# First merge step's gate products placed in the last prompt unit and the dilated decode; gates first in the merge; norm sums in other PSUM banks

## The chip, the cores and the metric

The kernel runs on one core of a Trainium2 chip. The metric is the device time of one execution in microseconds (us), the median of three runs. All matmuls are float32.

## What the reference computes

Two decoder layers, each over 256 prompt rows and 32 decode rows (8 samples of 4 new tokens). The kernel carries all 288 rows as one block of columns, so nearly every weight product is a matmul of 128 x 128 weights with 288 columns. Cut to what matters here, a layer is:

```
z = x @ w_in + b_in                      # queries, keys, values, merge gates
y_nsa = nsa_mixer(...)                   # 8 heads, 512 columns
y_dil = dilated_mixer(...)               # 3 groups of 4 heads, 256 columns
gm = sigmoid(g_merge)                    # last 2 x 1024 columns of z
mixed = gm[:, :, 0] * (y_nsa @ w_br_nsa) + gm[:, :, 1] * (y_dil @ w_br_dil)
x = layer_norm(ALPHA * x + mixed @ w_o, ln1_g, ln1_b)
h = square(relu(x @ w_ff1))
x = layer_norm(ALPHA * x + h @ w_ff2, ln2_g, ln2_b)
```

The gate columns of z need only the layer's input x. The branch products need y, which is there when attention has ended.

## The kernel before, in words

The five engines run programs of their own, written out by hand in one function (`build`), in fixed order, and they meet at semaphores that count up. Nothing plans the order at run time: an engine that reaches a wait stands until the count is there, and everything behind it in its program stands too. TensorE (`block.tensor`) does all products and transposes. ScalarE and VectorE take results out of PSUM. SyncE (`block.sync`) issues the weight loads one after another, each behind a wait for its buffer; GpSimd issues pages and values of the cache, and ScalarE issues stores and the copies of old cache rows into the new caches (`roll`, line 815).

**Weights** go through `w_ring`, four slots of 8 KB a partition. Unit u uses slot u % 4, and `free_of` (line 427) is SyncE's wait before it loads unit u: it waits for the last product that read the unit four before. Units 20 to 35 are the merge, 36 to 39 `w_o`, from 40 on the feed-forward weights. **Keys** of the decode caches go through `kv_ring`, two buffers of the same size.

**Around the change** the order on TensorE within a layer is this.

- Lines 1905 to 1916: the prompt units n = 16 to 23 of dilated attention. Each has scores (`p_scores`), transposes of the probabilities (`p_transpose`, line 1798) and values (`p_values`, line 1815). Between them run the 14 rounds of dilated decode keys (`d_round`, line 1878), which transpose keys out of `kv_ring`. VectorE's `dil_bias` (line 1356) comes before its `p_scale(23)`, so the transposes of unit 23 wait for it.
- Lines 1917 to 1947: the dilated decode. Ten transposes of its probabilities (`dlogit`) into banks 0 to 2, which ScalarE and VectorE copy to `pt`; then 160 recorded matmuls of probabilities with values into bank 6 (called P·V below); ScalarE copies the result out; four transposes put it in bank 7, and eight small copies by ScalarE put it into `yT`.
- Lines 1950 to 1960: the merge, a loop over p = 0 to 3 of 256 columns each. Within p there are four parts: w = 0 (`w_br_nsa`, 8 matmuls), w = 1 (`w_br_dil`, 4), w = 2 and w = 3 (the two gates, 16 each). Part w reads ring slot w and writes banks 2w and 2w + 1. ScalarE copies the branches and takes the tanh of the gates, VectorE joins them into `mixed` (lines 1396 to 1404).
- `wo` (line 1961): the eight output chunks of `mixed @ w_o`, for rows 0 to 143 (h = 0), then for rows 144 to 287 (h = 1), in banks 2 to 7. The sums of the layer norm (`mean`, `squares`, lines 1524 and 1538) are matmuls with ones, in banks 0 and 1 for the first norm (`LN_MEAN`, `LN_SQ`, line 80).
- `ff1_part` (line 1987): the first eight chunks of the feed-forward, by halves, in the order of `FF1_FIRST` = (4, 5, 6, 7, 2, 3, 0, 1), since banks 0 and 1 still hold the norm sums. Chunk c reads ring slot c // 2.

SyncE's order there: the last keys (line 638), the merge units 20 to 35 in order (lines 640 to 643), `w_o` (line 644), then `w_ff1`. The loop of the merge on TensorE before:

```
with pe.Fori(0, 4) as p:
    for w, (nk, k0, src) in enumerate(((4, 0, yT), (2, 4, yT), (KC, 0, xT), (KC, 0, xT))):
        pe.wait_ge(w_rdy[w].sem, ...)
        pe.wait_ge(mg_a.sem, mg_a.after(l, 4 * p + (w - 3)))
        for c in range(2):
            for k in range(nk):
                last = mm(bank(2 * w + c, 0, TOK), slot(w, nk, 256)[:, k, ...], src[:, k0 + k], k == 0, k == nk - 1)
        last.then_inc(mg_mm.sem, 1)
```

Of the kernel before, what the change touches and what calls it, by code (L numbers as in the profile page):

```python
# [79 lines left out]
LN_MEAN, LN_SQ = (0, 4), (1, 5)  # L80
HALF = (slice(0, TOK // 2), slice(TOK // 2, TOK))
FF1_FIRST = (4, 5, 6, 7, 2, 3, 0, 1)
# [6 lines left out]
NO_UNIT = (5, 8, 9, 19)  # L89
# [139 lines left out]
def build(nc, x_prompt, x_sample, cache_nsa_kv, cache_nsa_win, cache_dil_w128, cache_dil_w512, cache_dil_w2048,  # L229
# [11 lines left out]
    with ExitStack() as ctx:  # L241
# [134 lines left out]
        kv_rdy = [sig(f"kv_{s}", 16 * sum(KV_DMAS[s::2])) for s in range(2)]  # L376
        toep_rdy = [sig(f"dil_toep_{x}", 32) for x in range(2)]
# [42 lines left out]
        def _(sp):  # L420
# [6 lines left out]
            def free_of(l, u):  # L427
# [17 lines left out]
                elif v < U_MERGE:  # L445
                    b = v - (U_MERGE - W_SLOTS)
                    sp.wait_ge(dd_pv.sem, dd_pv.after(l, 4 * (b % 2) + b // 2 + 1))
                    sp.sem_inc(sp_steps, 1)
                elif v < U_WO:
                    sp.wait_ge(mg_mm.sem, mg_mm.after(l, v - U_MERGE + 1))  # L450
                    sp.sem_inc(sp_steps, 1)
                elif v < U_FF1:
                    sp.wait_ge(wo_mm.sem, wo_mm.after(l, 2 * (v - U_WO) + 2))
                    sp.sem_inc(sp_steps, 1)
                else:
                    raise ValueError(v)
# [10 lines left out]
            for l in range(layers):  # L467
# [19 lines left out]
                def kv_free(k):  # L487
                    v = k - 2
                    if v < 0:
                        sp.wait_ge(dd_pv.sem, dd_pv.after(l, v + 1))  # L490
                        sp.sem_inc(sp_steps, 1)
# [148 lines left out]
                for u in range(U_MERGE, U_MERGE + 4):  # L640
                    merge_unit(u)
                for u in range(U_MERGE + 4, U_WO):
                    merge_unit(u)
# [49 lines left out]
        def _(pool):  # L693
# [4 lines left out]
            for l in range(layers):  # L698
# [36 lines left out]
                def load_kv(k):  # L735

                    if k == 1:
                        pool.wait_ge(dd_pv.sem, dd_pv.after(l, 0))
# [55 lines left out]
        def _(act):  # L794
# [17 lines left out]
            for l in range(layers):  # L812
# [197 lines left out]
                A.copy(kt[:, 0, :], bank(6)).then_inc(dd_o.sem, 1)  # L1010
                act.wait_ge(dd_ot.sem, dd_ot.after(l, 1))

                o_v = bank(7).rearrange("p (q c b e s t) -> p q c b e s t", q=2, c=2, b=4, e=2, s=4)
# [64 lines left out]
        def _(dve):  # L1078
# [47 lines left out]
            for l in range(layers):  # L1126
# [279 lines left out]
                def wo_keep(h, c):  # L1406
                    done, cols = (wo_first, wo_mm)[h], HALF[h]
                    dve.wait_ge(done.sem, done.after(l, c + 1))
                    V.scalar_tensor_tensor(out=res[:, c, cols], in0=xT[:, c, cols], scalar=ALPHA, in1=bank(2 + c % 6, 0, TOK)[:, cols],  # L1409
# [55 lines left out]
        def _(pe):  # L1465
# [82 lines left out]
            for l in range(layers):  # L1548
# [376 lines left out]
                last.then_inc(dd_pt.sem, 1)  # L1925
                pe.wait_ge(dd_pta.sem, dd_pta.after(l, 1))
                pe.wait_ge(dd_ptd.sem, dd_ptd.after(l, 1))
                for par in range(2):
                    for q in range(4):
                        pe.wait_ge(dv_rdy[2 * q + par].sem, dv_rdy[2 * q + par].after(l, 64))  # L1930
                    for m in range(10):
                        for q in range(4):
# [3 lines left out]
                            out = bank(6, 256 * par, 256, pair.start, pair.stop)  # L1936
                            if m < 7:
                                mm(out, pt[:, m, pair], v[:, 256 * m:256 * m + 256], m == 0, False)
                            else:
                                a = 768 + 512 * (m - 7) + 256  # L1940
                                last = mm(out, pt[0:ND, m, pair], tm[0:ND, 2, a:a + 256], False, m == 9)
                                if m == 9:
                                    last.then_inc(dd_pv.sem, 1)
                pe.wait_ge(dd_o.sem, dd_o.after(l, 1))
                for k in range(4):
                    last = tr(bank(7, 128 * k, 128), kt[:, 0, 128 * k:128 * k + 128])
                last.then_inc(dd_ot.sem, 1)


                pe.wait_ge(dd_y.sem, dd_y.after(l, 1))  # L1950
                pe.wait_ge(dn_y.sem, dn_y.after(l, 2))
                pe.sem_inc(pe_steps, 1)
                with pe.Fori(0, 4) as p:
                    for w, (nk, k0, src) in enumerate(((4, 0, yT), (2, 4, yT), (KC, 0, xT), (KC, 0, xT))):
                        pe.wait_ge(w_rdy[w].sem, w_rdy[w].after(l, 16 * p + 16 * (w_loads(w, U_MERGE) + 1)))
                        pe.wait_ge(mg_a.sem, mg_a.after(l, 4 * p + (w - 3)))
                        for c in range(2):
                            for k in range(nk):
# [136 lines left out]
```

## Time and profile before

| What | us |
|---|---|
| Median of three runs | 1618.79 (1618.61 to 1619.01) |
| The profiled execution | 1611.5 |
| Span of the profiled execution, first to last instruction | 1609.8 |
| TensorE busy with matmuls | 1520.3 (94% of the span) |
| VectorE busy / ScalarE busy | 361.7 / 347.9 |

The profile shows one execution. An engine's timeline gives start, duration, engine, line, operation, out<-in and count of merged instructions, and in brackets how long the engine stood idle before and what ended it. One float32 matmul of the program shows as two records on TensorE (a float32 transpose as one). Because matmuls are pipelined, the duration of a row reaches a little into the next one; the distance between starts is the time that it took. Most matmuls and transposes have the line of a helper (1469 and 1473), so they are told apart by their operands. `arena` is a big buffer that many tiles share. The two layers lie at about 30 to 800 us and 800 to 1600 us, and the stretch around the change comes once in each.

### The profile page before, as it was taken

What the parts mean: (1) busy time and instruction counts of PE and PEld (TensorE: products, weight loads), DVE (VectorE), ACT (ScalarE), POOL (GpSimd) and SP (SyncE); (2) the same over time, 40 slices, a digit from 0 to 9 for tenths busy, and PEclk for the clock granted to TensorE, in tenths of its full rate; (3) what the DMA queues carried; (4) which work ended last, traced back from release to release, by engine and by line L of the source; (5) the groups of instructions that cost most, each with busy time, mean ns of one, the idle gap of its engine ahead of it and who ended that gap; (6) DMA issues with size and microseconds to landing.
All of it is one profiled execution on the core that took longest, in us unless ns stands there. A gap on an engine that the chain in (4) does not pass through costs nothing.

```text
span 1609.8 us, 24769 instructions
## 1 busy us (share of the span) xinstructions
PE 1520.3 (94%) x9164; PEld 1186.2 (74%) x9164; DVE 361.7 (22%) x1112; ACT 347.9 (22%) x932; POOL 158.8 (10%) x268
## 2 busy tenths in 40 slices
PE   8998999989899999999988989999889999999996
PEld 5656577767677987777975657777657789777786
DVE  1332234433011211100113242444220122110002
ACT  1132422234111211000123252222331112110003
POOL 2132420000000100000202424000000010000000
PEclk9999999999899999999999999999999999999999
DMA  9686568444355375565847454853716635655543
GB/s 265 155 194 156 150 216 279 151 159 144 126 187 182 106 257 186 187 232 187 244 127 178 121 153 123 291 180 122 239 56 205 215 105 173 243 192 183 196 162 132
DMA packets 212271, 288.06 MB, mean 179 GB/s; under 512 B 13781, under 2 KB 201383, under 8 KB 210888
## 3 DMA queue, kind: packets, MB, share of 16 engines
q1 hardware_dynamic: 194262, 189.01, 38.7%
q10 hardware_dynamic: 7858, 72.49, 12.0%
q0 software_dynamic: 10048, 25.19, 5.8%
q8 instruction: 65, 1.06, 0.3%
q14 instruction: 38, 0.31, 0.1%
HBM read 276.74 MB, written 72.49 MB: 217 GB/s over the span
## 4 chain that ended last, share of the span: by engine, by line
PE 82%; DMA 7%; issue 3%; DVE 2%; ACT 1%; POOLq 1%; SPq 1%; POOL 0%; ACTq 0%; DVEq 0%
PE psum L1469 77%; PE psum L1473 5%; DMA pages<-in_cache_nsa_kv 3%; DMA kv_ring<-in_cache_dil_w 1%; DMA w_ring<-in_w_in 1%; POOLq L702 1%; DMA w_ring<-in_w_ff 1%; ACT regrouped L838 1%; DMA arena<-in_x_sample 0%; DVE pt L1348 0%; SPq L506 0%; SPq L511 0%; DMA kv_ring<-in_cache_nsa_win 0%; SPq L471 0%; ACT xT L1052 0%
## 5 line engine op out<-in xcount | busy, mean ns | idle before, releaser
L1469 PE MATMUL psum<-arena,w_ring 128*128 128x144 f32 (+4 forms) x3584 | 684.1, 353 | 10.1 <-DVE arena L1404 4.8
L1469 PEld LDWEIGHTS psum<-arena,w_ring 128*128 128x128 f32 x3584 | 578.3, 190 | 110.5 <-DVE arena L1404 5.2
L1469 PE MATMUL psum<-xT,w_ring 128*128 128x288 f32 (+1 forms) x1472 | 358.4, 400 | 4.6 <-DMA w_ring<-in_w_in 4.6
L1469 PEld LDWEIGHTS psum<-xT,w_ring 128*128 128x128 f32 x1472 | 269.5, 191 | 80.1 <-issue 9.7
L779 POOL TENSOR_TENSOR arena<-arena 128x144 f32<-128x144 f32 x24 | 11.7, 487 | 653.6 <-DVE arena L1409 653.6
L1444 DVE TENSOR_TENSOR arena<-arena 128x288 f32 x64 | 29.3, 458 | 199.9 <-ACT arena L1062 199.9
L1062 ACT ACTIVATE arena<-psum 128x288 f32<-128x288 f32 x64 | 26.3, 410 | 197.3 <-PE psum L1469 197.3
L1195 DVE COPY arena<-psum 128x512 f32<-128x512 f32 x66 | 45.6, 692 | 78.4 <-PE psum L1473 78.2
L1469 PE MATMUL psum<-arena 64*128 64x128 f32 (+6 forms) x276 | 59.3, 342 | 0.0
L1447 DVE SCALAR_TENSOR_TENSOR arena<-arena,psum 128x288 f32<-128x288 f32 (+1 forms) x20 | 7.0, 390 | 223.0 <-PE psum L1469 223.0
L1473 PE MATMUL psum<-ident,regrouped 128*128 128x128 f32 (+1 forms) x300 | 48.3, 282 | 8.6 <-ACT regrouped L838 7.6
L1469 PE MATMUL psum<-pt,arena 128*64 128x128 f32 x336 | 49.2, 289 | 7.5 <-DVE pt L1353 3.4
L1469 PE MATMUL psum<-yT,w_ring 128*128 128x288 f32 x192 | 52.5, 434 | 3.9 <-ACT yT L1018 3.9
L1469 PE MATMUL psum<-kt,qn 128*32 128x256 f32 (+1 forms) x160 | 55.1, 434 | 0.0
L1400 DVE SCALAR_TENSOR_TENSOR arena<-arena 128x1152 f32<-128x1152 f32 x8 | 10.9, 1358 | 186.8 <-ACT arena L1036 186.8
L810 ACT ACTIVATE scrap<-eps_col 128x1 f32<-128x1 f32 x8 | 1.6, 202 | 232.5 <-issue 232.4
L715 POOL DMA_DIRECT2D pages<-in_cache_nsa_kv x64 | 38.3, 598 | 135.5 <-issue 51.7
L1469 PEld LDWEIGHTS psum<-yT,w_ring 128*128 128x128 f32 x192 | 39.2, 205 | 15.8 <-issue 4.3
L1469 PEld LDWEIGHTS psum<-arena 64*128 64x128 f32 (+3 forms) x276 | 40.0, 186 | 14.2 <-issue 11.9
L1473 PE MATMUL psum<-ident,logit 128*128 128x128 f32 (+2 forms) x252 | 41.2, 285 | 8.9 <-DVE logit L1275 5.2
L1473 PE MATMUL psum<-ident,kv_ring 128*128 128x128 f32 x288 | 41.4, 283 | 8.4 <-DMA kv_ring<-in_cache_dil_w 6.2
L838 ACT COPY regrouped<-pages 128x512 f32<-128x512 f32 x66 | 40.6, 618 | 38.4 <-DMA pages<-in_cache_nsa_kv 26.7
(206 smaller groups left out, 1214.7 us busy)
## 6 DMA issues: line engine op xcount, KB each, us to landing
w_ring<-in_w_ff SPq DMA_DIRECT2D x64, 1024.0 KB, 5.3
w_ring<-in_w_in SPq DMA_DIRECT2D x44, 1024.0 KB, 7.8
out<-in_cache_dil_w ACTq DMA_DIRECT2D x8, 1984.0 KB
pages<-in_cache_nsa_kv POOLq DMA_DIRECT2D x64, 192.0 KB, 4.5
pages<-in_cache_nsa_kv SPq DMA_DIRECT2D x64, 192.0 KB, 4.5
kv_ring<-in_cache_dil_w SPq DMA_DIRECT2D x20, 512.0 KB, 5.0
w_ring<-in_w_o SPq DMA_DIRECT2D x8, 1024.0 KB, 6.2
out<-in_cache_nsa_win ACTq DMA_DIRECT2D x8, 992.0 KB
```

What stands on the lines that cost most here:

```text
L702: v = pool.value_load(ptab[0:1, 8 * b + m:8 * b + m + 1], min_val=0, max_val=n_pool - 1)
L715: pool.dma_start(pages[64:128, s], page(b, 2 * m + 1)[:, :, 0:3].rearrange("o (q s) c h d -> (o q) s (c h d)", s=2)).then_inc(pg2_rdy[s].s ...
L779: P.tensor_tensor(relu[:, 0, cols], (res[:, 0] if c == 1 else relu[:, 0])[:, cols], res[:, c, cols], ALU.add).then_inc(added.sem, 1)
L810: A.activation(scrap[:, 0:1], eps_col[:, 0:1], function)
L838: A.copy(regr[:, p % 2].rearrange("p f (s d) -> p s f d", s=2), pages[:, s, :, 0:256].rearrange("p s (f d) -> p s f d", f=4)).then_inc(rg. ...
L1062: A.activation(relu[:, c % 2], bank(c, 0, TOK), ACT.Relu).then_inc(ff1_a.sem, 1)
L1195: V.tensor_copy(tcmp[:, :, :, col:col + 16], bank(p % 2).rearrange("p (f n j) -> p f j n", f=4, j=8)).then_inc(t_ev.sem, 1)
L1400: V.scalar_tensor_tensor(out=flat(a), in0=flat(t0), scalar=1.0, in1=flat(a), op0=ALU.add, op1=ALU.mult).then_inc(mg_x.sem, 1)
L1444: V.tensor_tensor(arena[:, bass.ds(j * (8 * TOK) + (3 * C8 + c * TOK), TOK)], relu[:, c % 2], relu[:, c % 2], ALU.mult).then_inc(ff1_d.sem, 1)
L1447: last = V.scalar_tensor_tensor(out=res[:, 2 * j + c, cols], in0=x1T[:, 2 * j + c, cols], scalar=ALPHA, in1=bank(banks + c, 0, TOK)[:, col ...
L1469: return T.matmul(out, w, x, start=start, stop=stop, **kw)
L1473: return T.transpose(out, in_, ident[0:n, 0:n])
```

## The change

The two gates of p = 0 leave the merge, each in two halves of 8 matmuls (`early_gate`). Their weights are loaded into the two buffers of `kv_ring`, after the last keys in them are transposed (rounds 12 and 13), so units 22 and 23 no longer exist. Gate w = 2 half 0 goes ahead of `p_transpose(23)`, half 1 behind it. Gate w = 3 half 0 goes behind the ten transposes of the dilated decode, half 1 behind P·V. To free banks 6 and 7 for gate w = 3, P·V moves to bank 3 and its four transposes to bank 2.

What is left of p = 0 is the two branches. For p = 1 to 3 the loop now does the gates first, w in the order 2, 3, 0, 1 (`MERGE_ORDER`); ScalarE follows the same order, and SyncE loads the units in the order (0, 1, 6, 7, 4, 5, 10, 11, 8, 9, 14, 15, 12, 13).

`wo` writes banks 4, 5, 0, 1, 2, 3, 4, 5 (`WO_BANK`), the first norm's sums go to banks 6 and 7, and `ff1_part` takes its chunks in plain order 0 to 7.

```diff
-LN_MEAN, LN_SQ = (0, 4), (1, 5)
+LN_MEAN, LN_SQ = (6, 4), (7, 5)
+MERGE_ORDER = (2, 3, 0, 1)
+WO_BANK = (4, 5, 0, 1, 2, 3, 4, 5)
-FF1_FIRST = (4, 5, 6, 7, 2, 3, 0, 1)
-NO_UNIT = (5, 8, 9, 19)
+NO_UNIT = (5, 8, 9, 19, 22, 23)
...
@@ free_of (SyncE) @@
-                elif v < U_MERGE:
-                    b = v - (U_MERGE - W_SLOTS)
+                elif v < U_MERGE or v in (U_MERGE + 2, U_MERGE + 3):
+                    b = v % W_SLOTS
                     sp.wait_ge(dd_pv.sem, dd_pv.after(l, 4 * (b % 2) + b // 2 + 1))
                     sp.sem_inc(sp_steps, 1)
                 elif v < U_WO:
-                    sp.wait_ge(mg_mm.sem, mg_mm.after(l, v - U_MERGE + 1))
+                    at = (v - U_MERGE) // 4 * 4 + MERGE_ORDER.index((v - U_MERGE) % 4)
+                    sp.wait_ge(mg_mm.sem, mg_mm.after(l, at + 1))
@@ SyncE, kv_free; GpSimd's load_kv(1) alike @@
                     if v < 0:
-                        sp.wait_ge(dd_pv.sem, dd_pv.after(l, v + 1))
+                        if l:
+                            sp.wait_ge(mg_mm.sem, mg_mm.after(l, 0))
@@ SyncE, after the last keys @@
-                for u in range(U_MERGE, U_MERGE + 4):
-                    merge_unit(u)
-                for u in range(U_MERGE + 4, U_WO):
-                    merge_unit(u)
+                for x, w in enumerate((6, 7)):
+                    sp.wait_ge(dkt.sem, dkt.after(l, 2 * dil_rounds(w).stop))
+                    sp.sem_inc(sp_steps, 1)
+                    col = MERGE_COL + x * D
+                    sp.dma_start(kvring[:, x].rearrange("p (k n) -> p k n", k=KC),
+                                 w_in[ld, :, col:col + 256].rearrange("o (k p) n -> p (o k) n", p=128)).then_inc(gate_rdy[x].sem, 16)
+                for u in (0, 1, 6, 7, 4, 5, 10, 11, 8, 9, 14, 15, 12, 13):
+                    merge_unit(U_MERGE + u)
@@ ScalarE, the merge @@
-                    for w in range(4):
-                        act.wait_ge(mg_mm.sem, mg_mm.after(l, 4 * p + (w + 1)))
-                        if w == 0:
+                    for at, w in enumerate(MERGE_ORDER):
+                        act.wait_ge(mg_mm.sem, mg_mm.after(l, 4 * p + (at + 1)))
+                        if at == 0:
@@ TensorE @@
+                merge_src = ((4, 0, yT), (2, 4, yT), (KC, 0, xT), (KC, 0, xT))
+                def merge_part(w, c, weights):
+                    nk, k0, x = merge_src[w]
+                    for k in range(nk):
+                        last = mm(bank(2 * w + c, 0, TOK), weights[:, k, 128 * c:128 * c + 128], x[:, k0 + k], k == 0, k == nk - 1)
+                    return last
+                def early_gate(x, c):
+                    if c == 0:
+                        pe.wait_ge(gate_rdy[x].sem, gate_rdy[x].after(l, 16))
+                    return merge_part(2 + x, c, kvring[:, x].rearrange("p (k n) -> p k n", k=KC))
                 for n in range(16, 24):
                     for r in ROUNDS_AT[n][0]:
                         d_round(r)
+                    if n == 23:
+                        pe.wait_ge(biased.sem, biased.after(l, 24))
+                        early_gate(0, 0)
                     p_transpose(n)
+                    if n == 23:
+                        early_gate(0, 1).then_inc(mg_mm.sem, 1)
...
-                pe.wait_ge(biased.sem, biased.after(l, 24))
-                pe.wait_ge(pt_d.sem, pt_d.after(l, 24))
                 pe.wait_ge(dd_prob.sem, dd_prob.after(l, 1))
-                pe.wait_ge(y_ev.sem, y_ev.after(l, 24))
...
                 last.then_inc(dd_pt.sem, 1)
+                pe.wait_ge(pt_d.sem, pt_d.after(l, 24))
+                early_gate(1, 0)
...
-                            out = bank(6, 256 * par, 256, pair.start, pair.stop)
+                            out = bank(3, 256 * par, 256, pair.start, pair.stop)
...
+                pe.wait_ge(y_ev.sem, y_ev.after(l, 24))
+                early_gate(1, 1).then_inc(mg_mm.sem, 1)
                 pe.wait_ge(dd_o.sem, dd_o.after(l, 1))
...
-                pe.wait_ge(dd_y.sem, dd_y.after(l, 1))
                 pe.wait_ge(dn_y.sem, dn_y.after(l, 2))
-                with pe.Fori(0, 4) as p:
...
+                for w in range(2):
+                    pe.wait_ge(w_rdy[w].sem, w_rdy[w].after(l, 16 * (w_loads(w, U_MERGE) + 1)))
+                    if w:
+                        pe.wait_ge(dd_y.sem, dd_y.after(l, 1))
+                    merge_part(w, 0, slot(w, merge_src[w][0], 256))
+                    merge_part(w, 1, slot(w, merge_src[w][0], 256)).then_inc(mg_mm.sem, 1)
+                with pe.Fori(1, 4) as p:
+                    for at, w in enumerate(MERGE_ORDER):
+                        first = w_loads(w, U_MERGE) + (1 if w < 2 else 0)
+                        pe.wait_ge(w_rdy[w].sem, w_rdy[w].after(l, 16 * p + 16 * first))
+                        pe.wait_ge(mg_a.sem, mg_a.after(l, 4 * p + (at - 3)))
...
@@ wo, and its keeping on VectorE @@
-                            pe.wait_ge(mg_a.sem, mg_a.after(l, 14 + c // 2))
+                            pe.wait_ge(mg_a.sem, mg_a.after(l, 13 + MERGE_ORDER.index(WO_BANK[c] // 2)))
...
-                        last = mm(bank(2 + c % 6, 0, TOK)[:, cols], slot(u, KC, 256)...
+                        last = mm(bank(WO_BANK[c], 0, TOK)[:, cols], slot(u, KC, 256)...
@@ ff1_part @@
-                    if c < 2 and h == 0:
+                    if c == 0 and h == 0:
+                        pe.wait_ge(wo_ev.sem, wo_ev.after(l, 12))
+                    if c > 5 and h == 0:
                         pe.wait_ge(ln_cen.sem, ln_cen.after(l, 8))
                         pe.wait_ge(ln_sd.sem, ln_sd.after(l, 2))
...
-                for at, c in enumerate(FF1_FIRST):
+                for c in range(8):
                     ff1_part(0, c)
-                    if at == 1:
+                    if c == 1:
                         mean(l, 0, 1)
-                    if at == 3:
+                    if c == 3:
                         squares(l, 0, 1)
```

## Rows read from the trace of the kernel before

**Rows 1.** The page, chain that ended last: shares of the span by engine.
```profile
PE 82%; DMA 7%; issue 3%; DVE 2%; ACT 1%; POOLq 1%; SPq 1%; POOL 0%; ACTq 0%; DVEq 0%
```

**Rows 2.** Timeline of TensorE, layer 0, from unit 22's values to the merge.
```profile
400.31 0.87 PE L1469 MATMUL psum<-pt,arena 128*64 128x128 f32 x6 [0.29 <-DVE pt L1348]
403.04 0.87 PE L1473 MATMUL psum<-ident,logit 128*128 128x128 f32 x6 [1.87 <-DVE logit L1339]
405.03 2.52 PE L1469 MATMUL psum<-pt,arena 128*64 128x128 f32 x12 [1.11 <-DVE pt L1353]
407.99 1.66 PE L1473 MATMUL psum<-ident,arena 128*128 128x128 f32 x10 [0.44 <-ACT yT L965]
...
420.61 0.66 PE L1473 MATMUL psum<-ident,kt 128*128 128x128 f32 x4 [0.78 <-ACT kt L1010]
423.21 9.07 PE L1469 MATMUL psum<-yT,w_ring 128*128 128x288 f32 x24 [1.94 <-ACT yT L1018]
```

**Rows 3.** Chain of waits in order of time, layer 0: start, us, what (P·V).
```profile
410.59 9.36 PE psum L1469 x160
```

**Rows 4.** Timeline of TensorE, layer 0: merge from p = 0's gates, then `wo`.
```profile
432.11 15.68 PE L1469 MATMUL psum<-xT,w_ring 128*128 128x288 f32 x64
447.63 5.98 PE L1469 MATMUL psum<-yT,w_ring 128*128 128x288 f32 x24
453.45 15.68 PE L1469 MATMUL psum<-xT,w_ring 128*128 128x288 f32 x64
...
515.69 18.40 PE L1469 MATMUL psum<-arena,w_ring 128*128 128x144 f32 x148 [2.40 <-DVE arena L1404]
```

**Rows 5.** Timeline of TensorE, layer 1, the same stretch.
```profile
1184.97 0.87 PE L1469 MATMUL psum<-pt,arena 128*64 128x128 f32 x6 [0.29 <-DVE pt L1348]
...
1279.31 15.68 PE L1469 MATMUL psum<-xT,w_ring 128*128 128x288 f32 x64
...
1298.86 20.07 PE L1469 MATMUL psum<-arena,w_ring 128*128 128x144 f32 x148 [2.40 <-DVE arena L1404]
```

**Rows 6.** Windows: us, busy of PE, PEld, DVE, ACT, POOL, PEclk, DMA share, GB/s.
```profile
392.00:400.00 8.00, 7.81 (x180) 6.13 (x178) 3.18 (x9) 3.18 (x8) 0.00 (x0) 1.00 0.01 2
...
405.00:408.00 3.00, 2.53 (x13) 2.16 (x13) 0.78 (x2) 0.26 (x1) 0.00 (x0) 0.56 0.00 0
...
412.00:420.00 8.00, 7.83 (x140) 3.84 (x132) 0.00 (x0) 0.03 (x1) 0.00 (x0) 1.00 0.21 68
...
423.20:428.60 5.40, 5.39 (x11) 3.87 (x12) 0.00 (x0) 0.00 (x0) 0.00 (x0) 0.50 1.08 402
...
1207.80:1211.00 3.20, 3.13 (x7) 2.29 (x8) 0.00 (x0) 0.00 (x0) 0.00 (x0) 0.51 1.26 439
...
1298.80:1302.20 3.40, 3.34 (x17) 3.35 (x18) 0.30 (x1) 0.00 (x0) 0.00 (x0) 0.63 0.20 66
...
515.60:519.00 3.40, 3.31 (x27) 3.31 (x28) 0.64 (x3) 0.00 (x0) 0.00 (x0) 1.00 0.20 68
```

**Rows 7.** Timeline of TensorE, layer 0: last keys but one, unit 21's values.
```profile
391.64 1.09 PE L1473 MATMUL psum<-ident,kv_ring 128*128 128x128 f32 x8
...
393.50 1.52 PE L1469 MATMUL psum<-pt,arena 128*64 128x128 f32 x12 [0.19 <-DVE pt L1353]
```

**Rows 8.** Weight loads at 420.4, 504.1, 496.4, 791.2: count, KB, us to landing.
```profile
w_ring<-in_w_in SPq DMA_DIRECT2D x1, 1024.0 KB, 5.5
...
w_ring<-in_w_o SPq DMA_DIRECT2D x1, 1024.0 KB, 5.0
...
w_ring<-in_w_o SPq DMA_DIRECT2D x1, 1024.0 KB, 8.4
...
w_ring<-in_w_in SPq DMA_DIRECT2D x1, 1024.0 KB, 19.0
```

**Rows 9.** Timeline of TensorE, both layers: start of the feed-forward.
```profile
549.83 4.19 PE L1469 MATMUL psum<-arena,w_ring 128*128 128x144 f32 x32 [1.54 <-DMA w_ring<-in_w_ff]
...
1334.62 4.19 PE L1469 MATMUL psum<-arena,w_ring 128*128 128x144 f32 x32 [1.49 <-DMA w_ring<-in_w_ff]
```

More of the change, by code:

```diff
@@ L376, in build @@
         kv_rdy = [sig(f"kv_{s}", 16 * sum(KV_DMAS[s::2])) for s in range(2)]
+        gate_rdy = [sig(f"early_gate_{x}", 16) for x in range(2)]
         toep_rdy = [sig(f"dil_toep_{x}", 32) for x in range(2)]
@@ L489, in kv_free @@
                     if v < 0:
-                        sp.wait_ge(dd_pv.sem, dd_pv.after(l, v + 1))
-                        sp.sem_inc(sp_steps, 1)
+                        if l:
+                            sp.wait_ge(mg_mm.sem, mg_mm.after(l, 0))
+                            sp.sem_inc(sp_steps, 1)
                     elif v < 6 and v % 3 == 0:
@@ L639, in _ @@
                     load_kv(k)
-                for u in range(U_MERGE, U_MERGE + 4):
-                    merge_unit(u)
-                for u in range(U_MERGE + 4, U_WO):
-                    merge_unit(u)
+                for x, w in enumerate((6, 7)):
+                    sp.wait_ge(dkt.sem, dkt.after(l, 2 * dil_rounds(w).stop))
+                    sp.sem_inc(sp_steps, 1)
+                    col = MERGE_COL + x * D
[3 more added lines that the diff above has]
+                    merge_unit(U_MERGE + u)
                 for i in range(4):
@@ L737, in load_kv @@
                     if k == 1:
-                        pool.wait_ge(dd_pv.sem, dd_pv.after(l, 0))
+                        pool.wait_ge(mg_mm.sem, mg_mm.after(l, 0))
                     elif k in (2, 5):
@@ L1009, in _ @@
                 act.wait_ge(dd_pv.sem, dd_pv.after(l, DB))
-                A.copy(kt[:, 0, :], bank(6)).then_inc(dd_o.sem, 1)
+                A.copy(kt[:, 0, :], bank(3)).then_inc(dd_o.sem, 1)
                 act.wait_ge(dd_ot.sem, dd_ot.after(l, 1))
-                o_v = bank(7).rearrange("p (q c b e s t) -> p q c b e s t", q=2, c=2, b=4, e=2, s=4)
+                o_v = bank(2).rearrange("p (q c b e s t) -> p q c b e s t", q=2, c=2, b=4, e=2, s=4)
                 for q in range(2):
@@ L1408, in wo_keep @@
                     dve.wait_ge(done.sem, done.after(l, c + 1))
-                    V.scalar_tensor_tensor(out=res[:, c, cols], in0=xT[:, c, cols], scalar=ALPHA, in1=bank(2 + c % 6, 0, TOK)[:, cols],
+                    V.scalar_tensor_tensor(out=res[:, c, cols], in0=xT[:, c, cols], scalar=ALPHA, in1=bank(WO_BANK[c], 0, TOK)[:, cols],
                                            op0=ALU.mult, op1=ALU.add).then_inc(wo_ev.sem, 1)
@@ L1943, in _ @@
                                     last.then_inc(dd_pv.sem, 1)
+                pe.wait_ge(y_ev.sem, y_ev.after(l, 24))
+                early_gate(1, 1).then_inc(mg_mm.sem, 1)
                 pe.wait_ge(dd_o.sem, dd_o.after(l, 1))
                 for k in range(4):
-                    last = tr(bank(7, 128 * k, 128), kt[:, 0, 128 * k:128 * k + 128])
+                    last = tr(bank(2, 128 * k, 128), kt[:, 0, 128 * k:128 * k + 128])
                 last.then_inc(dd_ot.sem, 1)
-                pe.wait_ge(dd_y.sem, dd_y.after(l, 1))
                 pe.wait_ge(dn_y.sem, dn_y.after(l, 2))
                 pe.sem_inc(pe_steps, 1)
-                with pe.Fori(0, 4) as p:
[L1954 to L1958, printed above, removed]
-                                last = mm(bank(2 * w + c, 0, TOK), slot(w, nk, 256)[:, k, 128 * c:128 * c + 128], src[:, k0 + k], k == 0, k == nk - 1)
-                        last.then_inc(mg_mm.sem, 1)
+                for w in range(2):
[9 more added lines that the diff above has]
+                        pe.wait_ge(mg_a.sem, mg_a.after(l, 4 * p + (at - 3)))
+                        merge_part(w, 0, slot(w, merge_src[w][0], 256))
+                        merge_part(w, 1, slot(w, merge_src[w][0], 256)).then_inc(mg_mm.sem, 1)
                 def wo(h, c):
@@ L1972, in wo @@
                             pe.wait_ge(mg_d.sem, mg_d.after(l, k // 2 + 1))
-                        last = mm(bank(2 + c % 6, 0, TOK)[:, cols], slot(u, KC, 256)[:, k, 128 * (c % 2):128 * (c % 2) + 128], mixed[:, k, cols], k == 0, k == KC - 1)
+                        last = mm(bank(WO_BANK[c], 0, TOK)[:, cols], slot(u, KC, 256)[:, k, 128 * (c % 2):128 * (c % 2) + 128], mixed[:, k, cols], k == 0, k == KC - 1)
                     last.then_inc((wo_first, wo_mm)[h].sem, 1)
@@ L1993, in ff1_part @@
                     for k in range(KC):
-                        if k % 2 == 0 and c == (FF1_FIRST[0], 0)[h]:
+                        if k % 2 == 0 and c == 0:
                             pe.wait_ge(ln_out.sem, ln_out.after(l, 4 * h + k // 2 + 1))
```

## The prediction

> **What bounds the kernel now.** I read the page's chain first: the work that ended last is TensorE's for 82% of the span, DMA 7% [rows 1]. So time is won only where TensorE stands idle or runs at the low clock, and every moved product counts at its full length. Next I read TensorE's timeline from the end of unit 22's values (400.31 + 0.87 = 401.18 in layer 0) to the merge. It is the thinnest stretch of the layer: TensorE waits 1.87 us for VectorE's scaling of unit 23, 1.11 for its copies, 0.44 and 0.78 for ScalarE, and 1.94 for the copies into `yT` [rows 2]. Behind those holes stands a second loss. Unit 23's 12 value records take 2.52 us where unit 21's same 12 take 1.52 [rows 2, 7], and the merge's first 24 records take 432.11 - 423.21 = 8.90 us where p = 1's take 453.45 - 447.63 = 5.82 [rows 2, 4]. The windows tell why: the granted clock is 0.56 from 405 to 408 and 0.50 from 423.2 to 428.6, the lower of TensorE's two levels (1.2 of 2.4 GHz), both times just after idle; layer 1 shows 0.51 at the merge's start [rows 6]. From there to its end the merge is dense: one p takes 453.45 - 432.11 = 21.34 us, of which 15.52 are gates (447.63 - 432.11) [rows 4].
>
> **The change, part by part.** I count from the end of unit 22's values to the start of the record behind the last merge product, called T before and T' after.
>
> *Gates in the holes.* Each half gate is a quarter of p's 15.52 us, 3.88 us. They add no work, they leave p = 0. The new stretch at full clock is four halves 15.52; the transposes of unit 23 0.87 [rows 2]; its values 1.52, at unit 21's price [rows 7]; ten transposes 1.36, at the keys' 1.09 for eight [rows 7]; P·V 9.36 [rows 3]; four transposes 0.66 [rows 2]; p = 0's branches 5.82; and three p, 64.02 [rows 4]. That is 99.1 us, plus some 0.1 for handoffs. Before it was 432.11 + 64.02 + 15.52 - 401.18 = 110.5 in layer 0, and from 1185.84 to 1279.31 + 15.52 = 1294.83, 109.0, in layer 1 [rows 5]. The gain is 11.3 and 9.8 us. In layer 0 the holes are the 6.14 us named above and 0.94 ahead of P·V (407.99 + 1.66 to 410.59 [rows 2, 3]), 7.1 in all; the rest, 4.2, is clock. With holes of the same length layer 1's clock share is 2.7.
>
> Does anything open a new hole? Half 0 of gate 2 begins at 401.2, and VectorE's probabilities are there at 403.04, so unit 23's transposes now come about 2.0 us later, at 405.1. VectorE's copies (the 1.11 us hole) lie under half 1, the copies before P·V under the third half, ScalarE's copy after P·V under the fourth, and the copies into `yT` (1.94 us) under the 3.88 us of branch 0, which reads none of them. Where one of these covers is missing, its hole returns at the size in rows 2. The value products come some 5 us later than before, but only TensorE's own order waits for them.
>
> *The gate weights.* SyncE sends the first 1 MB when round 12's keys are transposed, at 391.64 + 1.09 = 392.7 [rows 7]. A like load landed in 5.5 us, one beside a cache copy in 8.4 [rows 8]: 398.2 to 401.1, needed at 401.2. The DMA share there is 0.01 [rows 6], so I take 5.5: no wait. The second has 10 us more. On SyncE's queue the loads stand behind the last keys, which must come first anyhow, and ahead of the merge units, whose buffers P·V frees far later: nothing queued is late. Units 6 and 7, p = 1's gates, go out at the end of P·V; TensorE needs unit 6 only 3.88 + 0.66 + 5.82 = 10.4 us later, twice the 5.5. The waits for the next layer's first keys (SyncE and GpSimd) pass, since the merge ended hundreds of us before: zero. The moved banks were read out before they are written again, and the waits at their new places (`pt_d`, `y_ev`) name work already done: zero. ScalarE meets p = 0's gates finished, so it catches up.
>
> *The start of `wo`.* This part costs. Ring slot 0 used to be free with p = 3's first part, 17.5 us before T (15.52 + 1.94, a third of 5.82). Now branch 0 is the last but one, and unit 36 goes out only 1.94 us before the merge ends; behind it on SyncE's queue stand units 37 to 39, whose slots may long be free. A lone `w_o` load took 5.0 us [rows 8], so the weights come at about T' + 3.3 (with 0.2 for the matmul's end and the signal). Before, 12 records (1.47 us) ran inside the wait for VectorE and the rest from 515.69, which is T + 4.04, as if `wo` had begun at T + 2.57 [rows 4]. VectorE's part is unchanged and now lies under these 12 records. Loss 0.75 us a layer; 4.1 if the load takes 8.4. Nothing below zero is to be had, as VectorE sets the floor. The Trainium skill (DMA: Bandwidth & Descriptors, section Anatomy of one DMA) gives a fitted 2.0 us plus bytes over 436 GB/s for a transfer issued by GpSimd, an estimate of 4.4 us here; by that the loss would be 0.15 a layer and the sum 1.2 us better. The measured 5.0 on this queue decides.
>
> *Clock there.* The idle time at `wo` grows from 2.40 to some 3.3 us, and is no longer broken by 12 records. The same 2.40 us left the clock at 1.00 in layer 0 and at 0.63 for 3.4 us in layer 1 [rows 4 to 6], which made 20.07 - 18.40 = 1.67 us. With the longer idle I take the drop in both layers: 1.7 more in layer 0, nothing in layer 1. Bounds: from -1.7 (none in either) to 4.5 (both as long as at 423.2, 8.90 - 5.82 = 3.08 each, less the 1.67 already paid). The Trainium skill (TensorE: Matmul & The Clock Gate, section HAM oscillation) says that a wait for DMA between bursts sends the clock down and is paid at every burst. By it the drop comes in both layers, as taken; layer 0's row so far speaks against it, and going by that row alone the sum would be 3.4 us better.
>
> *Feed-forward.* It begins with chunk 0, whose slot is the first that `wo` frees, instead of chunk 4. The waits of 1.54 and 1.49 us for a `w_ff1` load [rows 9] go; slots 2 and 3 are wanted 8 and 12 us later, more than a load's 5 us. Chunks 6 and 7 now wait for the norm sums as 0 and 1 did, at the same place. Gain 3.0.
>
> **Sum:** 11.3 + 9.8 - 1.5 - 1.7 + 3.0 = 20.9 us. The profiled execution, 1611.5 us (span 1609.8), would be 1590.6. The median of the runs is 7.3 us higher than it; I take the same difference off the median: 1618.8 - 20.9 = 1597.9.
>
> **The rivals.**
> 1. *The clock does not come back.* The holes are filled but low stretches appear elsewhere, say between the tiny products ahead of unit 23 and P·V. Then the 4.2 + 2.7 = 6.9 us are missing: 1604.8. For it: the low rows follow idle at no fixed distance. Against: P·V, light as its products are, runs at 1.00 from 412 to 420 [rows 6].
> 2. *The four `w_o` loads share the DMA engines instead of coming in turn.* At T' unit 36 has had 1.9 of its 5.0 us. If the other 3.1 went at a quarter of the rate, it would land 9.3 us later; as some part of 3.1 is delay and not transfer, I price the middle, 4.7 a layer: 1607.3. Against: loads of one queue, half a microsecond apart, where the first took 5.5, close to a lone 5.0 [rows 8].
> 3. *Slower: `w_o` caught behind a cache copy.* In the trace a weight load issued at 791.2 beside large cache copies took 19.0 us [rows 8]. With that price `wo` begins 14.0 us later in each layer, 28 us: 1625.9. It decides once unit 36 takes 5.0 + 10.5 = 15.5 us or more. For it: ScalarE sends a `roll` in each p. Against: p = 3's goes out some 20 us before T', and the next after the norm.
> 4. *The change doesn't do what it says:* the gate weights land late, and TensorE stands at the first half instead of in the holes. At 13 us to landing, between 8.4 and 19.0 [rows 8], it waits 4.5 us a layer: 1606.9. The idle DMA speaks against it.
>
> **How the numbers follow.** My forecast has 0.60 (its own range is 1594 to 1601: clock at `wo`, and the loads). Rival 1 has 0.17, rival 2 0.10, rival 4 0.06, rival 3 0.04; 0.03 is left for a time about as before, where several of the costs meet. The range reaches from 1593.5 (no drop at `wo` in either layer, 1594.5, and one us for small handoffs) to 1609, which holds rivals 1, 2 and 4 at their prices; two of them at once are left out. About 0.2% (3.2 us) is what a measurement here can tell from no change; faster by more than that has 0.92, within it 0.03, slower 0.05.
>
> **What would show it.** Right: TensorE without holes from unit 22's values to the end of the merge, clock 1.00 there, about 99 us between; the first `wo` record 3.3 us behind the merge, released by a `w_o` load, with a low clock after it; no wait for `w_ff1`. Wrong: idle in front of the first half gate or of the p = 1 gates, low clock within the stretch, or waits inside `wo` for units 37 to 39.

## The result and the profile after

On the first occasion the changed kernel ran in 1591.54 us, the median of four executions (1587.57 to 1598.98), against 1618.7 for the kernel before (four, 1615.66 to 1619.01): a ratio of 0.9842, 95% interval 0.9821 to 0.9864. That is 27 us less where 20.9 were forecast, and 2 us below the low end of the range. The profiled execution took 1587.57 us (span 1585.9), which is 23.9 below the profiled one of before.

TensorE's timeline of the changed kernel, layer 0, answers to [rows 2 to 4]. The half gates are the rows that read `kv_ring`, 16 records each.

```profile
400.35 0.87 PE L1477 MATMUL psum<-pt,arena 128*64 128x128 f32 x6 [0.29 <-DVE pt L1356]
401.14 4.15 PE L1477 MATMUL psum<-xT,kv_ring 128*128 128x288 f32 x16
405.13 0.82 PE L1481 MATMUL psum<-ident,logit 128*128 128x128 f32 x6
405.78 4.05 PE L1477 MATMUL psum<-xT,kv_ring 128*128 128x288 f32 x16
409.76 1.52 PE L1477 MATMUL psum<-pt,arena 128*64 128x128 f32 x12
411.21 1.31 PE L1481 MATMUL psum<-ident,arena 128*128 128x128 f32 x10
412.36 4.05 PE L1477 MATMUL psum<-xT,kv_ring 128*128 128x288 f32 x16
...
425.51 4.15 PE L1477 MATMUL psum<-xT,kv_ring 128*128 128x288 f32 x16
429.49 0.60 PE L1481 MATMUL psum<-ident,kt 128*128 128x128 f32 x4
429.93 5.99 PE L1477 MATMUL psum<-yT,w_ring 128*128 128x288 f32 x24
435.75 15.68 PE L1477 MATMUL psum<-xT,w_ring 128*128 128x288 f32 x64
...
493.95 5.98 PE L1477 MATMUL psum<-yT,w_ring 128*128 128x288 f32 x24
503.12 19.87 PE L1477 MATMUL psum<-arena,w_ring 128*128 128x144 f32 x160 [3.19 <-DMA w_ring<-in_w_o]
```

No row between 401 and the end of the merge carries a wait any more. Unit 23's values are back at 1.52 us (2.52 in [rows 2]) and the merge's first 24 records at 435.75 - 429.93 = 5.82 (8.90). T' is 493.95 + 5.82 = 499.77. What is new is the 3.19 us for `w_o` at 503.12.

Where the difference lies is read from the windows, cut at the same pieces of work in both kernels: up to unit 22's values, from there to the merge's end, `w_o` up to the feed-forward, and the rest up to the next layer's same place. The columns are those of [rows 6]. First the changed kernel, all seven pieces; then the four of the kernel before that answer to the change.

```profile
0.00:401.20 401.20, 372.22 (x2405) 265.65 (x2405) 130.65 (x449) 121.39 (x333) 69.13 (x117) 0.99 0.68 193
401.20:499.90 98.70, 98.70 (x545) 74.61 (x544) 11.91 (x21) 16.32 (x45) 0.00 (x0) 1.00 0.43 140
499.90:537.00 37.10, 33.91 (x277) 33.88 (x277) 11.22 (x27) 7.39 (x17) 5.86 (x12) 1.00 0.57 184
537.00:1173.00 636.00, 610.75 (x3755) 476.18 (x3753) 154.21 (x499) 147.24 (x397) 73.59 (x120) 0.99 0.60 186
1173.00:1271.60 98.60, 98.60 (x544) 74.58 (x544) 11.87 (x21) 16.32 (x45) 0.00 (x0) 1.00 0.43 140
1271.60:1310.50 38.90, 35.70 (x278) 35.59 (x278) 11.22 (x27) 7.39 (x17) 5.86 (x12) 0.96 0.56 178
1310.50:1585.90 275.40, 261.91 (x1370) 220.02 (x1368) 30.97 (x70) 32.05 (x78) 5.09 (x7) 0.99 0.54 184
```

```profile
401.20:511.70 110.50, 103.45 (x545) 78.25 (x546) 11.86 (x21) 16.32 (x45) 0.00 (x0) 0.95 0.51 171
511.70:549.80 38.10, 34.20 (x277) 33.76 (x275) 11.51 (x28) 7.58 (x17) 5.84 (x12) 1.00 0.35 114
...
1185.80:1294.80 109.00, 101.94 (x545) 77.21 (x545) 11.92 (x21) 16.33 (x45) 0.00 (x0) 0.97 0.52 173
1294.80:1334.60 39.80, 35.94 (x277) 35.48 (x275) 11.51 (x28) 7.58 (x17) 5.84 (x12) 0.96 0.34 108
```

Between the two profiles the stretch gave 11.8 and 10.4 us, and `w_o` with the start of the feed-forward 1.0 and 0.9: 24.1 in all, which is the whole difference of the spans. TensorE's busy time equals the stretch's length, 98.70 of 98.70 and 98.60 of 98.60, and its clock went from 0.95 and 0.97 to 1.00. So this pair of executions gained 3.2 us more than the sum of 20.9, and the medians another 3 us that no stage of the two profiles holds. The experiments were made to find where those come from.

### The profile page after: what moved, and what is told of

Its sections match the earlier page's. It is cut to its first block, busy times and chain, and to the rows that moved or that the text cites. A ratio compares the mean times of both kernels' runs of the same rounds, so it can differ in the third digit from the quotient of the medians.

```text
span 1585.9 us, 24738 instructions
## 1 busy us (share of the span) xinstructions
PE 1511.8 (95%) x9164; PEld 1180.5 (74%) x9164; DVE 362.0 (23%) x1112; ACT 348.1 (22%) x932; POOL 159.5 (10%) x268
## 4 chain that ended last, share of the span: by engine, by line
PE 85%; DMA 6%; issue 4%; POOLq 1%; DVE 1%; ACT 1%; SPq 1%; POOL 0%; ACTq 0%; DVEq 0%
PE psum L1477 79%; PE psum L1481 6%; DMA pages<-in_cache_nsa_kv 3%; POOLq L710 1%; DMA w_ring<-in_w_in 1%; DMA kv_ring<-in_cache_dil_w 1%; DMA w_ring<-in_w_o 1%; ACT regrouped L846 0%; DMA arena<-in_x_sample 0%; DVE pt L1356 0%; SPq L510 0%; DMA kv_ring<-in_cache_nsa_win 0%; ACT xT L1060 0%; SPq L515 0%; DVE logit L1283 0%
## 5 line engine op out<-in xcount | busy, mean ns | idle before, releaser
L1477 PE MATMUL psum<-xT,w_ring 128*128 128x288 f32 (+1 forms) x1344 | 327.9, 400 | 4.9 <-DMA w_ring<-in_w_in 4.9
L1477 PEld LDWEIGHTS psum<-xT,w_ring 128*128 128x128 f32 x1344 | 245.6, 192 | 74.6 <-issue 10.0
L1481 PEld LDWEIGHTS psum<-ident,kv_ring 128*128 128x128 f32 x288 | 31.5, 143 | 23.7 <-issue 8.9
L1481 PEld LDWEIGHTS psum<-ident,regrouped 128*128 128x128 f32 (+1 forms) x300 | 32.4, 139 | 21.2 <-ACT regrouped L846 18.9
L1477 PE MATMUL psum<-yT,w_ring 128*128 128x288 f32 x192 | 47.9, 406 | 0.0
```

Of the source, the lines that this page charges most:

```text
L1477: return T.matmul(out, w, x, start=start, stop=stop, **kw)
L1481: return T.transpose(out, in_, ident[0:n, 0:n])
```

## The experiments

**Theory A:** the holes are filled, and the clock that fell behind them stays up; what is beyond the forecast is scatter of the clock elsewhere. **Rival B:** the surplus comes from loads that land earlier, or from the order of the merge. **Rival C:** the low clock has nothing to do with these holes.

### The changed kernel twice more

No edit.

> The changed kernel unaltered, to see what its executions scatter by. Theory A (holes filled, and TensorE's granted clock kept up): 20 to 28 us below the kernel before, and the span of each execution follows its mean granted clock: between 0.992 and 0.986 lie 0.6% of 1590 us, some 9.5 us. Rival B (the excess over the forecast comes from loads that land earlier somewhere else): spans scatter without regard to the clock.

> The changed kernel unaltered once more, as the measure for its neighbours. Theory A: 18 to 24 us below the kernel before; at full clock its span would be within 3 us of what the earlier profiles give, span times granted clock, 1571 to 1575 us. Rival B: span times clock scatters as much as the span.

Measured: 1598.72 us (five executions, 1594.68 to 1604.43), ratio to the kernel before 0.9878 (0.9858 to 0.9898); and 1598.87 us (six, 1594.81 to 1603.44), ratio 0.9874 (0.9846 to 0.9901). With 1617.39 and 1619.92 for the kernel before on these occasions that is 19.7 and 20.4 us, by the ratios. Over all occasions the median is 1597.44 us for 15 executions of the changed kernel (1587.57 to 1604.43) and 1618.8 for 38 of the kernel before (1611.2 to 1626.57). Three of the first occasion's four executions are the lowest of these 15. The first repeat was expected 20 to 28 us below the kernel before and misses that by 0.3 us; the second lies within its 18 to 24.

The windows of the first repeat's profile (1604.43 us, the slowest of all 15), cut as above:

```profile
0.00:406.40 406.40, 375.98 (x2405) 267.78 (x2406) 130.71 (x450) 121.22 (x334) 68.82 (x117) 0.98 0.68 190
406.40:505.10 98.70, 98.67 (x544) 74.55 (x544) 11.83 (x21) 16.28 (x45) 0.00 (x0) 1.00 0.42 140
505.10:545.20 40.10, 36.92 (x277) 36.92 (x278) 11.21 (x27) 7.39 (x17) 5.83 (x12) 0.91 0.53 169
545.20:1190.10 644.90, 618.46 (x3755) 482.32 (x3753) 154.31 (x499) 146.88 (x397) 73.48 (x120) 0.98 0.58 184
1190.10:1288.70 98.60, 98.60 (x545) 74.63 (x544) 11.92 (x21) 16.30 (x45) 0.00 (x0) 1.00 0.43 140
1288.70:1327.50 38.80, 35.61 (x276) 35.46 (x276) 11.21 (x27) 7.40 (x17) 5.84 (x12) 0.96 0.55 178
1327.50:1602.80 275.30, 261.78 (x1371) 220.07 (x1369) 30.96 (x70) 31.94 (x78) 5.09 (x7) 0.99 0.54 185
```

The changed stretch is the same to the tenth, 98.70 and 98.60, at 1.00. The 16.9 us between the two spans lie elsewhere: 5.2 before the stretch, 8.9 between the layers' stretches and 3.0 at layer 0's `w_o`, each with a lower granted clock. TensorE's busy time is longer by 3.8, 7.7 and 3.0 us there; the other 2.6 us are waits. The record has span and clock of all 15 executions of the changed kernel. The spans reach from 1585.9 to 1602.8 us and the clocks from 0.992 down to 0.980, and span times clock lies between 1569.1 and 1574.9: 5.8 us of scatter where the spans have 16.9. So the scatter follows the clock, as theory A had it, and rival B's scatter without regard to the clock is out for this kernel. The expected 1571 to 1575 us were a little high: the second repeat's six products lie between 1569.2 and 1573.0.

The product is a rough check and no law. For the 34 executions of the kernel before whose clock is on record it scatters by 8.9 us where the spans scatter by 15.4. In a later experiment, the one with the wait for `w_o` filled, it scatters by 8.5 us where the spans lie within 4.2.

### The holes opened again

```diff
-                    if n == 23:
-                        pe.wait_ge(biased.sem, biased.after(l, 24))
-                        early_gate(0, 0)
                     p_transpose(n)
-                    if n == 23:
-                        early_gate(0, 1).then_inc(mg_mm.sem, 1)
...
-                early_gate(1, 0)
...
-                early_gate(1, 1).then_inc(mg_mm.sem, 1)
...
+                pe.wait_ge(dd_y.sem, dd_y.after(l, 1))
                 pe.wait_ge(dn_y.sem, dn_y.after(l, 2))
+                for x in range(2):
+                    early_gate(x, 0)
+                    early_gate(x, 1).then_inc(mg_mm.sem, 1)
```

(and the four waits of the kernel before ahead of the decode's transposes)

> The changed kernel with its four half gates of p = 0 moved behind the dilated decode, in front of the two branches, and the old waits in the decode; the loads through the key ring, the gates-first order, the banks and the feed-forward order stay. Theory A: the 7 us of holes per layer and the clock loss behind them return, 18 to 24 us above the changed kernel, so within 5 us of the kernel before (less 3.0 for the feed-forward, plus 1.5 for the late w_o). Rival B (the order of loads or the gates-first order carries the gain): stays at least 12 us below the kernel before.

Measured: 1620.0 us (12 executions), ratio 1.0016 (0.9994 to 1.0038): the kernel before. TensorE's timeline of this run, layer 0:

```profile
406.55 0.87 PE L1481 MATMUL psum<-ident,logit 128*128 128x128 f32 x6 [1.87 <-DVE logit L1347]
408.54 2.82 PE L1477 MATMUL psum<-pt,arena 128*64 128x128 f32 x12 [1.11 <-DVE pt L1361]
...
428.80 17.19 PE L1477 MATMUL psum<-xT,kv_ring 128*128 128x288 f32 x64 [1.59 <-ACT yT L1026]
```

The 1.87 and 1.11 us are those of [rows 2], and the slow records behind them are back: 2.82 us for unit 23's values, and 17.19 for 64 gate records that take 15.68 at full clock. The place of the half gates, with the waits that go with it, is worth 1.0016 - 0.9878 = 0.0138, or some 22 us; it was expected to be 18 to 24. The new loads, the gates-first order, the banks and the feed-forward order together are worth nothing that can be told without it (1.0016 holds 1 within its interval), where the forecast's terms for them come to -1.5 - 1.7 + 3.0 = -0.2 us. This is rival B's end.

### Spare products in the holes of the kernel before

```diff
+                def spare(b, n):
+                    for _ in range(n):
+                        mm(bank(b, 0, TOK), ident[:, :], xT[:, 0])
...
+                    if n == 23:
+                        spare(0, 3)
                     p_transpose(n)
+                    if n == 23:
+                        spare(0, 2)
...
                 last.then_inc(dd_pt.sem, 1)
+                spare(4, 1)
...
+                spare(4, 1)
                 pe.wait_ge(dd_o.sem, dd_o.after(l, 1))
...
                 last.then_inc(dd_ot.sem, 1)
+                spare(4, 3)
```

> The kernel before, with ten spare products a layer (one 128 x 128 by 288 product each, results never read) put into the holes: three ahead of unit 23's transposes, two ahead of its values, one ahead of P.V, one ahead of the decode's four transposes, three ahead of the merge. No useful work is moved, so the holes stay as long as they were, 0.3 to 0.5 us of each still idle. Theory A: the clock stays at its higher level through unit 23's values and the merge's start, and the time falls by the clock's part alone, 7 us (its price in the profiled execution) up to 12 if usual executions lose more. Rival C (the low clock does not come from these holes): no change, 0 to 2 us either way.

Measured: 1610.1 us (12 executions), ratio 0.9961 (0.9943 to 0.9978), 6.3 us below the kernel before. Its timeline, layer 0; the rows with `xT,ident` are the spare products:

```profile
402.54 1.72 PE L1469 MATMUL psum<-xT,ident 128*128 128x288 f32 x6
404.48 0.87 PE L1473 MATMUL psum<-ident,logit 128*128 128x128 f32 x6 [0.22 <-DVE logit L1339]
405.19 1.14 PE L1469 MATMUL psum<-xT,ident 128*128 128x288 f32 x4
406.47 1.52 PE L1469 MATMUL psum<-pt,arena 128*64 128x128 f32 x12
...
423.28 6.08 PE L1469 MATMUL psum<-yT,w_ring 128*128 128x288 f32 x24 [0.49 <-ACT yT L1018]
```

Nothing useful is moved, and counted from unit 22's values the first two holes end when they did, yet unit 23's values take 1.52 us instead of 2.52, and the merge's first 24 records 6.08 instead of 9.07 [rows 2]; layer 1 shows 1.52 and 6.08 too. The forecast's price of the clock was 4.2 + 2.7 = 6.9. The 6.3 us fall just short of the 7 to 12 that were expected of this run, though its interval (3.6 to 9.2) reaches into them. Rival C falls: the low clock came from these holes.

### The old feed-forward order

```diff
-LN_MEAN, LN_SQ = (6, 4), (7, 5)
+LN_MEAN, LN_SQ = (0, 4), (1, 5)
-WO_BANK = (4, 5, 0, 1, 2, 3, 4, 5)
+WO_BANK = (2, 3, 4, 5, 6, 7, 2, 3)
+FF1_FIRST = (4, 5, 6, 7, 2, 3, 0, 1)
...
-                    if c == 0 and h == 0:
-                        pe.wait_ge(wo_ev.sem, wo_ev.after(l, 12))
-                    if c > 5 and h == 0:
+                    if c < 2 and h == 0:
```

(and the loop over `FF1_FIRST` as before)

> The changed kernel with the old feed-forward order, the old banks of w_o and the old banks of the norm sums. Theory A: the two waits of about 1.5 us for a w_ff1 load return, so 3.0 us above the changed kernel. Rival: 0 us, if the wait at the start of w_o or the clock hides it; over 6 us if the banks matter by themselves.

Measured: 1602.88 us (six executions), ratio 0.9924 (0.9899 to 0.9948), 4 us above the changed kernel's 1598.72 of the same occasion by the medians, and some 7 by the ratios. The intervals meet at 0.9898 and 0.9899, so the time confirms the 3.0 in direction and not in size, and by itself it does not exclude the rival that the banks cost something too. The waits of this run's trace give the size:

```profile
PE psum L1478 <- DMA w_ring<-in_w_ff: 3.2, 2, 1.8
```

Two waits of 3.2 us together (engine, line, what it waited for: us in all, times, longest), which the changed kernel does not have. In layer 0 it is 291.5 us from the first record of `w_o` to the small transpose that ends the layer (503.86 to 795.37), and 289.4 in the first profile of the changed kernel (503.12 to 792.53). The 2.1 us between them are hardly more than the longer of the two waits, 1.8, so in this pair of profiles the banks by themselves cost a few tenths at most.

### The first `w_o` weights in the key ring

```diff
+                    if u in (10, 8):
+                        i = (10, 8).index(u)
+                        sp.wait_ge(mg_mm.sem, mg_mm.after(l, i + 1))
+                        sp.dma_start(kvring[:, i].rearrange("p (k n) -> p k n", k=KC),
+                                     w_o[ld, :, 256 * i:256 * i + 256]...).then_inc(gate_rdy[i].sem, 16)
-                for i in range(4):
+                for i in range(2, 4):
                     u = U_WO + i
...
+                    weights = slot(u, KC, 256) if c > 3 else kvring[:, c // 2].rearrange("p (k n) -> p k n", k=KC)
```

(with the waits of slots 0 and 1 and of the next layer's keys to match)

> The changed kernel with the first two w_o units loaded into the key ring in the middle of the merge, once the half gates have read it, instead of into ring slots 0 and 1 at its end. Theory A (w_o begins when its weights land): the wait of 3.2 us for w_o in each layer shrinks to the wait for VectorE, broken by 12 records as in the kernel before: 0.8 to 1.0 us a layer, so 1.6 to 2 us below the changed kernel, and up to 3 us more if the clock falls less often. Rival (the loads collide with merge weights and cache copies): waits for w_in or w_br inside the merge, no gain or a loss.

Measured: 1598.61 us (six executions), ratio 0.9870 (0.9840 to 0.9900), beside 1598.87 for the changed kernel: not to be told apart. The trace shows the gain all the same:

```profile
501.54 1.63 PE L1486 MATMUL psum<-arena,kv_ring 128*128 128x144 f32 x12
505.28 6.64 PE L1486 MATMUL psum<-arena,kv_ring 128*128 128x144 f32 x52 [2.11 <-DVE arena L1421]
...
1284.70 8.31 PE L1486 MATMUL psum<-arena,kv_ring 128*128 128x144 f32 x52 [2.11 <-DVE arena L1421]
```

The releaser is VectorE again, and `w_o` begins as if at 505.28 - 1.47 = T' + 2.3 instead of T' + 3.35, so 1.1 us a layer. But 2.11 us of idle still let layer 1's clock fall (8.31 us for the 52 records that took 6.64 in layer 0), and the rest is lost in the scatter. The expected 1.6 to 2 us were neither shown nor refuted by the time. The rival's waits for merge weights inside the merge do not appear in the trace.

### The same, and the wait filled

```diff
-                for c in range(KC):
+                for ks in (range(KC - 2), range(KC - 2, KC)):
+                    for c in range(3):
+                        wo(0, c, ks)
+                for c in range(3, KC):
                     wo(0, c)
```

> The same, and w_o's first three chunks start with their first six products each (36 records, 4.4 us), which need only mixed columns that are long there; the two products that need p = 3 follow. Theory A: no idle time between merge and w_o, 3.2 us a layer and up to 3 us of clock: 6 to 12 us below the changed kernel. Rival: something else is late at once (VectorE's merging, the norm sums), and less than 3 us come.

Measured: 1589.07 us (six executions, 1588.15 to 1592.31), ratio 0.9811 (0.9787 to 0.9835): 9.8 us below the changed kernel of the same occasion and below both kernels of this case. The timeline across the end of the merge in layer 0, and the first of `w_o` in layer 1:

```profile
495.35 5.98 PE L1486 MATMUL psum<-yT,w_ring 128*128 128x288 f32 x24
501.17 8.00 PE L1486 MATMUL psum<-arena,kv_ring 128*128 128x144 f32 x64
...
1278.61 8.00 PE L1486 MATMUL psum<-arena,kv_ring 128*128 128x144 f32 x64
```

495.35 + 5.82 is 501.17, so TensorE goes on without a pause, at full clock in both layers (8.00 us for 64 records). The wait of 3.35 us a layer makes 6.7, and the drop of 1.7 in layer 1 brings it to 8.4; the rest of the 9.8 would be layer 0's drop where it comes, which is an estimate and not told apart from scatter. It lies within the expected 6 to 12. The prediction's "VectorE sets the floor" for the start of `w_o` held only for the order of products as it stood: the first six products of a chunk need no late column.

### Spare products ahead of `w_o`

```diff
+                pe.wait_ge(mg_a.sem, mg_a.after(l, 14))
+                for _ in range(6):
+                    mm(bank(6, 0, TOK), ident[:, :], xT[:, 0])
                 for c in range(KC):
                     wo(0, c)
```

> The changed kernel with six spare products (2.9 us, results never read) in the wait for w_o. The wait stays as long, TensorE is busy in it. Theory A (the low clock behind it comes from the idle time): w_o's first part at full clock in both layers, 1.7 us below the changed kernel on average, 0 to 3 a layer. Rival: no change of the clock there.

Measured: 1594.39 us (six executions), ratio 0.9843 (0.9816 to 0.9870), 4.5 us below the changed kernel's 1598.87 where 1.7 were expected; the intervals overlap, so the time alone does not show the gain. The trace, layer 0, and layer 1's `w_o`; for comparison the next fences have `w_o` in the changed kernel: layer 0 in the first repeat, then layer 1 in the first profile, then layer 1 in the second repeat:

```profile
500.12 3.07 PE L1477 MATMUL psum<-xT,ident 128*128 128x288 f32 x12
503.47 19.87 PE L1477 MATMUL psum<-arena,w_ring 128*128 128x144 f32 x160 [0.27 <-DMA w_ring<-in_w_o]
...
1278.70 19.87 PE L1477 MATMUL psum<-arena,w_ring 128*128 128x144 f32 x160 [0.44 <-DMA w_ring<-in_w_o]
```

```profile
508.28 22.84 PE L1477 MATMUL psum<-arena,w_ring 128*128 128x144 f32 x160 [3.21 <-DMA w_ring<-in_w_o]
```

```profile
1274.91 21.54 PE L1477 MATMUL psum<-arena,w_ring 128*128 128x144 f32 x160 [3.19 <-DMA w_ring<-in_w_o]
```

```profile
1284.17 21.54 PE L1477 MATMUL psum<-arena,w_ring 128*128 128x144 f32 x160 [3.20 <-DMA w_ring<-in_w_o]
```

With TensorE busy in the wait the 160 records take 19.87 us in both layers. Behind an idle wait of the same length they took 19.87, 22.84 and 19.87 in layer 0 (first profile and the two repeats), and 21.54 in layer 1 of all three. So the drop comes from the idle wait. In layer 1 it came every time; in layer 0 it came in one of the three profiles. No run shows what sets the layers apart.

## Why the prediction was right in its steps and wrong in its range

- **The stretch:** 99.2 us from unit 22's values to the merge's end; 98.7 and 98.6 measured, without a hole, in all three profiles of the changed kernel. The half microsecond is the remainder of two errors in the sum. It took the short pieces at their rows' durations, which reach into the next row: unit 23's transposes at 0.87 us, where 405.78 - 405.13 = 0.65 was measured, the ten transposes at 1.36 for 412.36 - 411.21 = 1.15, the last four at 0.66 for 429.93 - 429.49 = 0.44; with the values and P·V this is 0.9 too much. And each half gate took 3.98 us (409.76 - 405.78) instead of 3.88, 0.4 too little in all. With the 0.1 that was given to handoffs this makes the difference.
- **The split between holes and clock:** 6.9 us were given to the clock; the spare products, which give back the clock alone, brought 6.3 (3.6 to 9.2 by the interval). The changed stretch has a clock of 1.00, so rival 1 is out there.
- **The gate weights:** taken as landed in time. SyncE sent the first at 392.87, the half gate at 401.14 did not wait. Rival 4 is out.
- **The start of `w_o`:** forecast at T' + 3.3 behind a load of 5.0 us. Measured T' + 3.35, and the chain of the changed kernel has the load:

```profile
498.09 4.99 DMA w_ring<-in_w_o
```

  The fitted formula of the Trainium skill (DMA: Bandwidth & Descriptors, Anatomy of one DMA), which it gives for transfers issued by GpSimd, would have had it at an estimated 4.4. Units 37 to 39 were sent about half a microsecond apart once the merge had ended, and landed 6.3, 9.3 and 11.9 us after they were sent: in turn, and keeping nobody waiting (160 records in a row, 19.87 us). Rivals 2 and 3 are out.
- **The clock at `w_o`:** 1.7 us more in layer 0 was the taken value, and nothing more in layer 1. Layer 1 had the drop in all three profiles, as it had before. In layer 0 it was 0, 3.0 and 0: the bounds held it, and the value taken was layer 1's. The 1.7 that did not come are part of the 3.2 us by which the profiled pair beat the sum; the rest is the half microsecond of each stretch and some 0.2 a layer at `w_o` and the start of the feed-forward. The rule of the Trainium skill (TensorE: Matmul & The Clock Gate, HAM oscillation), as the prediction put it, that a wait for DMA sends the clock down at every burst, agrees with layer 1's three rows and with one of layer 0's three.
- **The feed-forward:** 3.0 forecast; the waits are gone, and 3.2 when put back.
- **The step that failed** is the one behind the sum: "I take the same difference off the median". It treated one execution's distance to the median, 7.3 us, as a fixed thing, and gave the range only the bounds of the stretch's own terms. Measured, the changed kernel's median lay 4.0 us above its profiled execution on the first occasion (1591.54 - 1587.57), 5.7 below it on the second and 2.3 above it on the third. Of the 6.3 us by which the first occasion beat the sum (27.2 for 20.9), about half is the profiled pair's and about half this distance. Executions of one kernel lie up to 17 us apart, mostly by the clock granted far from the change. On the first occasion the median stood at 1591.5; on the two later ones at 1598.7 and 1598.9, and over 15 executions at 1597.4, where 1597.9 was forecast. By the ratios the change is worth 19.7 and 20.4 us there, of 20.9 forecast, each with 3 to 4.5 us either way, so that they agree with it to about a microsecond is in part luck. The range should have had this scatter added at both ends.

What stays open is why the clock stood higher in the other stages on the first occasion. It does not look like a chance draw of four from the 15: the first occasion's executions have the four highest clocks, 0.986 to 0.992, and the eleven later ones 0.980 to 0.985. The profiled execution of the kernel before has 0.986 as well, above all 34 of its later ones (0.976 to 0.985); its other executions of the first occasion have no clock on record, and their median was not lower. The record gives chip 1 for the second occasion, chip 15 for the third and none for the first, so a difference between chips is neither shown nor ruled out. The change does not touch those stages, and no run tried their holes.

## What to carry to other kernels

A hole on the busiest engine has two prices, its length and the low clock behind it; here they were 7.1 and up to 4.2 us a layer, so work that is independent and ready (a gate that needs only the layer's input) is worth moving into even one-microsecond holes. A reordering that frees a buffer later moves a load onto the path: look at which slot the next stage's first weights use, and use the buffer that lies idle (the key ring) and the products that need no late input to cover what is left. Before a forecast is set against a median of few executions, ask how far the same kernel's executions lie apart. Where their clocks differ, span times granted clock is a rough check (5.8 us of scatter for 16.9 here, but 8.5 for 4.2 in the run with the wait filled); the windows of the changed stretch are the better one.

## What was not expected of the hardware

Products whose results nobody reads made a kernel faster: ten in each layer, 6.3 us. Six ahead of `w_o` kept the clock up in both layers in the profiled execution. An idle time of about 3.2 us was followed by the low clock in layer 1 of all three profiles of the changed kernel and in layer 0 of one. The clock granted in stages that the change does not touch makes most of the 17 us by which executions of the changed kernel differ: their spans times their clocks agree within 5.8 us.
